# Moving the weights 16 bytes against the tensors that stream past them, on TensorE, in one diffusion-transformer layer

## The reference, cut to what matters

```python
proj = h @ w_in                        # 2048 -> 3072, latent and context tokens
u_f, u_x, u_g = jnp.split(proj, [D_FOURIER, D_FOURIER + D_LRU], axis=-1)
x_c = depthwise_conv(u_x, conv_w, conv_b, LRU_CONV // 2)
...
y = jnp.concatenate([y_fourier, y_lru], axis=-1) @ w_out      # 2048 -> 2048
x = x + gt1 * rms_norm(y, g_mix_post)
hx2 = modulate(rms_norm(x, g_ffn_pre), sh2, sc2)
up = depthwise_conv(hx2 @ w_up, conv_w, conv_b, FFN_CONV // 2)   # 2048 -> 11264
g, v = jnp.split(up, 2, axis=-1)
x = x + gt2 * rms_norm((jax.nn.gelu(g, approximate=True) * v) @ w_down, g_ffn_post)
```

## The kernel before, in words

| tensor | first byte | remainder |
|---|---|---|
| h_hi / h_lo | 20,192 / 52,960 | 224 |
| w_raw and w_lo / w_hi | 85,728 / 106,208 | 224 |
| hc_lo / hc_hi | 126,688 / 143,072 | 224 |
| t_lo / t_hi | 126,688 / 138,976 | 224 |
| sums1_lo / sums1_hi | 155,360 / 193,632 | 224 / 96 |
| act_hi / act_lo | 204,512 / 212,704 | 224 |
| xc and g parts (recurrence gates) | 165,600 and up / 190,176 and up | 224 |
| eo parts (weights) / m parts (stream), Fourier | 159,456 and up / 176,000 and up | 224 / 384 |
| p parts (weights) / tok parts (stream), Fourier | 184,192 and up / 167,744 and up | 384 / 320 to 376 |

## Time and profile before

### The profile page before, as it was taken

How to read it: one execution, slowest core, us unless ns; L and a number is a source line. 1 busy time by engine, 2 the same in 40 slices (tenths; PEclk the granted TensorE clock), 3 DMA queues, 4 the chain that set the end, 5 groups by cost and what they waited for, 6 DMA issues and landing times.

```text
span 2103.6 us, 28297 instructions
## 1 busy us (share of the span) xinstructions
PE 2071.2 (98%) x11682; PEld 1772.5 (84%) x11682; DVE 1529.6 (73%) x2202; ACT 811.6 (39%) x1077; POOL 78.7 (4%) x145
## 2 busy tenths in 40 slices
PE   7999999999999999999999999999999999999998
PEld 4678887888777888888889898898988889888887
DVE  5567978876988975867767676676766758577577
ACT  5346577543323442423324233332333424233243
POOL 0000000001110000000000000000000000000002
PEclk9999999999999999999999999999999999999999
DMA  9953424434876523333333333334233333232343
GB/s 394 408 204 110 154 96 161 137 109 173 323 277 225 181 90 134 100 128 111 110 130 101 138 103 103 129 101 140 100 120 121 100 130 100 91 101 101 100 172 109
DMA packets 86193, 311.19 MB, mean 148 GB/s; under 512 B 9456, under 2 KB 13552, under 8 KB 84016
## 3 DMA queue, kind: packets, MB, share of 16 engines
q1 hardware_dynamic: 67824, 243.09, 32.7%
q0 software_dynamic: 17424, 65.50, 9.1%
q10 hardware_dynamic: 816, 0.79, 0.1%
HBM read 300.95 MB, written 8.39 MB: 147 GB/s over the span
## 4 chain that ended last, share of the span: by engine, by line
PE 80%; DVE 2%; ACT 1%; DMA 1%; issue 0%; DVEq 0%; ACTq 0%
PE bank L988 26%; PE bank L990 26%; PE bank L989 26%; DMA w_raw<-in_stream 1%; PE bank L1099 1%; DVE acc L2167 0%; PE bank L1284 0%; DVE w_lo L1532 0%; ACT w_hi L602 0%; PE bank L1313 0%; PE bank L1194 0%; DVE acc L2139 0%; ACT lru_u L698 0%; DVE cv L1544 0%; DVE x L2193 0%
## 5 line engine op out<-in xcount | busy, mean ns | idle before, releaser
L988 PE MATMUL bank<-h_hi,w_hi 128*128 128x512 f32 (+1 forms) x1968 | 711.2, 361 | 4.2 <-ACT y_lru L671 1.2
L989 PE MATMUL bank<-h_lo,w_hi 128*128 128x512 f32 (+1 forms) x1968 | 708.6, 360 | 0.0
L990 PE MATMUL bank<-h_hi,w_lo 128*128 128x512 f32 (+1 forms) x1968 | 707.2, 359 | 0.0
L1532 DVE TENSOR_TENSOR w_lo<-w_raw,w_hi 128x1024 fp32r<-128x1024 f32 x260 | 316.0, 1222 | 157.9 <-ACT w_hi L602 157.8
L988 PEld LDWEIGHTS bank<-h_hi,w_hi 128*128 128x128 f32 x1968 | 372.3, 189 | 63.6 <-issue 11.9
L602 ACT ACTIVATE w_hi<-w_raw 128x1024 fp32r<-128x1024 f32 x260 | 273.0, 1056 | 389.1 <-DMA w_raw<-in_stream 389.0
L990 PEld LDWEIGHTS bank<-h_hi,w_lo 128*128 128x128 f32 x1968 | 372.1, 189 | 56.6
L989 PEld LDWEIGHTS bank<-h_lo,w_hi 128*128 128x128 f32 x1968 | 372.3, 189 | 49.0
L988 PE MATMUL bank<-act_hi,w_hi 128*128 128x512 f32 (+1 forms) x688 | 265.0, 385 | 1.7 <-DVE acc L2139 1.5
L990 PE MATMUL bank<-act_hi,w_lo 128*128 128x512 f32 (+1 forms) x688 | 264.2, 384 | 0.0
L989 PE MATMUL bank<-act_lo,w_hi 128*128 128x512 f32 (+1 forms) x688 | 264.2, 384 | 0.0
(11 more groups left out here) (340 smaller groups left out, 2711.4 us busy)
## 6 DMA issues: line engine op xcount, KB each, us to landing
w_raw<-in_stream SPq DMA_DIRECT2D x340, 512.0 KB, 3.5
ada_raw<-in_adabg POOLq DMA_DIRECT2D x112, 512.0 KB, 4.3
ada_raw<-in_ada SPq DMA_DIRECT2D x64, 512.0 KB, 13.5
x<-in_x_t SPq DMA_DIRECT2D x4, 1024.0 KB, 8.4
acc<-in_adabg SPq DMA_DIRECT2D x8, 512.0 KB, 6.1
x<-in_x_t POOLq DMA_DIRECT2D x4, 1024.0 KB, 9.4
x_kept_d<-x SPq DMA_DIRECT2D x4, 1024.0 KB, 5.6
c<-in_ctx_t SPq DMA_DIRECT2D x2, 1024.0 KB, 14.3
```

The source lines that it names most:

```text
L988: t.matmul(out, w, v, start=start, stop=False)
L989: t.matmul(out, w, v_l, start=False, stop=False)
L990: return t.matmul(out, w_l, v, start=False, stop=stop)
L1532: v.tensor_tensor(lo_unit(n), raw_unit(n), hi_unit(n).bitcast(F32), ALU.subtract).then_inc(lo_done, 1)
```

## The change

The tensors of the ring become flat, each with 8 values (32 bytes) more than five slots, and every use of a slot starts 4 values (`SKIP`, 16 bytes) further up. A space of 480 bytes before `w_hi` brings its slots to the remainder of `w_lo`'s. What lies behind `w_hi` on the left side moves up by 544 bytes, which is 512 and 32. `gap_to_act` shrinks from 1664 to 128 bytes. `ada_rows`, a buffer of 1 KB for the conditioning rows, becomes a view of `csq0`, the buffer of squares of the context tokens, so that `ada0_raw` moves down by that 1 KB less the 544.

```diff
+SKIP = 4
...
-        w_raw, w_lo = twice(ctx, "w_raw", "w_lo", [P, RING, UNIT])
-        w_hi = sbuf(ctx, "w_hi", [P, RING, UNIT], F32R)
+        w_raw, w_lo = twice(ctx, "w_raw", "w_lo", [P, RING * UNIT + 8])
+        sbuf(ctx, "gap_to_high", [P, 120])
+        w_hi = sbuf(ctx, "w_hi", [P, RING * UNIT + 8], F32R)
...
-                ada_rows = sbuf(s0, "ada_rows", [P, 2 * P])
+                ada_rows = csq0[:, 0, :]
...
-            sbuf(s, "gap_to_act", [P, 416])
+            sbuf(s, "gap_to_act", [P, 32])
...
-                return w_raw[:, SLOT[n], :]
+                return w_raw[:, ds(SKIP + UNIT * SLOT[n], UNIT)]
...
-                return w_hi[:, SLOT[n], :]
+                return w_hi[:, ds(SKIP + UNIT * SLOT[n], UNIT)]
...
-                return w_lo[:, SLOT[n], :]
+                return w_lo[:, ds(SKIP + UNIT * SLOT[n], UNIT)]
...
-            return w_raw[:, SUMS0, 0:NSUM], w_hi[:, SUMS0, 0:NSUM], w_lo[:, SUMS0, 0:NSUM]
+            return tuple(t[:, ds(SKIP + UNIT * SUMS0, NSUM)] for t in (w_raw, w_hi, w_lo))
...
-                a.activation(ada_rows[:, :], rows_bank(c)[:, 0:2 * P], ACT.Copy).then_inc(rows_copied, 1)
+                a.activation(ada_rows, rows_bank(c)[:, 0:2 * P], ACT.Copy).then_inc(rows_copied, 1)
```

## The result

The changed kernel takes 2121.44 us (median of three: 2120.11, 2121.44, 2125.28); its ratio to the kernel before is 1.0078, 95% interval 1.006 to 1.0096.

A forecast was written before the change was run, and what follows sets the result against it. TensorE's row of matmuls, busy 98%, was taken as the bound: 2 ns less on 9216 matmuls, other edits 0, made 2105.4 - 18.4 = 2087.0 us, plus 0.6 to the median, written 2088; range 2030 to 2128.

The forecast's parts named there:

- The failed step: Extended a 2 ns gain from short matmuls to the 6192 long ones, within 18 us less for 9216 matmuls.
- row (a): Last 18 matmuls of seven_products, one weight tensor 128 bytes lower: 118.3 ns each against 120, 1.7 ns on the mean.
- (b): Six 512-column steps right behind the matmuls with sums take 230 ns each, 3 ns above the steady 227.
- All other edits at 0 us: Ring passes, transfers and moved conditioning rows were taken as 0 us; the transfers' bounds were 0 and +10 us.
- the surplus: About 13 ns per matmul beyond its columns, absent at half clock; all of it would be 123 us over 9216 matmuls.
- the lost rhythm: 6192 long matmuls lose 3 to 5 ns each, wandering from 230: 2120 to 2132 us; chance 0.30 with settling higher.
- settled higher: Rhythm settles one short-kind surplus higher; half of 13.3 ns up would be +61 us; shares chance 0.30 with the lost rhythm.
- No change: Distance matters only above 16 bytes, or the rhythm settles again at 120 and 227 ns: 2106 us; chance 0.19.
- The large gain: Stream and loads stop meeting; half or all of the surplus goes, 61 or 123 us: 2044 or 1983 us; chance 0.20.

The follow-up runs named there:

- d0: The changed kernel's layout with weights at distance 0 from all streams, as in the kernel before; 2106.47 us, ratio 1.0007 to the kernel before.
- m128: As d0, but with weights 128 bytes below all streams; 2136.34 us in one run.
- p16: As d0, but with weights 16 bytes above all streams, act included; 2136.64 us, ratio 1.0146 to the kernel before.
- m64act: As d0, but with weights 64 bytes below h, hc and t, and act kept at distance 0; 2095.05 us, ratio 0.9948 to the kernel before.

## Why the prediction was wrong

**The failed step** is the one that took row (a), the 2 ns that short matmuls with sums gained at 128 bytes, over to the long ones ("I extend it to the long matmuls, for which the rows show only a worse value in transition; this is the weakest step"). It made 2 x 6192 = 12 us less of what became 6.1 ns more for each long matmul on `h` in the steady state, 0.1 ns for each on `act` in four down projections and 1.6 in six, and 14.7 us more in all. The row that was at hand, (b), pointed the other way; it was set aside since the steps had settled after six. But (b) was such a transition back to distance 0. At +16 there is nothing at 227 to return to: the steps settle at 233.3 within the first matmuls and stay.

**What held.** TensorE's pace was the bound, and the starts of successive matmuls told all. The short matmuls: 119.9 to 118.1 ns, the 2 ns forecast for them, 0.13 us in each of 40 turns. All other edits at 0 us: d0's ratio is 1.0007 (0.9998 to 1.0016), landing 3.5 us and 1055 ns a pass. That the surplus exists at the full clock only: m128's six steps of 427 ns. The first 125 us were 1.2 us shorter, for another reason than the change: seven steps of 427 ns at half the clock, five of them in the earlier trace rows, have no counterpart in the trace after, whose granted clock from 43 to 45.4 us is 1.00, and 7 x 0.2 is 1.4 us. With the stretch at 493 us, the trace before lost about 3 us to the clock that the trace after didn't, so the change costs nearer to 18 us than to 14.7 at an equal clock (an estimate).

**The rival that came true** is the lost rhythm, 2120 to 2132 us for a measured 2121.4. Its place was half right: 4224 long matmuls on `h`, not the 1968 on `act`. Its picture was half right too: the steps are uneven, from 231 to 235 ns, but they don't wander; they repeat in a pattern whose mean is 233.3, which is the other half of its case ("settled higher"). Its price of 3 to 5 ns was short of 6, and the two errors made up for each other. Neither it nor any other case gave the sign of the distance a part, though the change had both signs, +16 for `h` and -16 for `act`, `hc` and `t`; by p16 both at +16 would have cost 30 us.

**No change** fell by the trace and by p16 against d0. The Trainium skill, page "SBUF — State Buffer", section "Who interferes with whom", has TensorE's two read ports independent and never waiting. The runs disagree: with nothing but the weights' place moved by 16 bytes, a long step goes from 227.2 to 233.3 ns. The same page could be right in that neither port waits on another engine; no run here looked at that.

**The large gain** fell as well. Half of it exists for short steps, 113.4 of 120, but at 64 bytes and not at 16, and long ones never went under 226.7. The even rhythms, in which all steps are alike to 1 ns, have 113.3, 120 and 226.7 ns, which are 17, 18 and 34 times 6.67 ns: 16 cycles of 2.4 GHz, in which 64 bytes of a stream pass. 233.3 is 35 times as much, but it, 228.3, 229 and 117.3 to 118.7 are means of steps of several lengths (at -128 bytes 229 and 238 ns in turn), and these single steps are no multiples. So the surplus of 13.3 ns, which the prediction read as 32 cycles for 32 pieces of 16 bytes, may come in portions of 6.67, one or two of them in the even rhythms; the uneven ones leave it open. By the formula of the Trainium skill, page "TensorE: Matmul & The Clock Gate", section "Back-to-back issue gap", a long step would be 216 ns, as the prediction took it; the section gives that for an isolated matmul, and for a stream in which each has its load about 131 ns. The least here was 226.7, so neither holds in this kernel.

**Shown and open.** Shown: the distance between weights and stream sets the steady step, with its sign, for each length in its own way, and 256 bytes more make no difference at distance 0; the place of both together does not (32 bytes at distance 0, 64 bytes at -64); at -64 short matmuls have two steady rhythms, and what precedes decides; at -16 long ones have two. Argued only: that stream and weight load meet at parts of the 256 bytes and that one waits out a portion of 64 bytes; no run shows the meeting itself. Why +16 and -16 differ, and +64 and -64 for long steps alone, stays open, as do distances of 32, 96 and 160 bytes, and whether one-column matmuls in the right place could set the good rhythm on purpose, or taking them out keep it; none of these was tried.

## What to carry to other kernels

When TensorE runs without gaps and each matmul loads its own weights, compare the starts of successive matmuls for each shape, and treat the remainders of weights and stream by 256 as a parameter to be scanned in steps of 16 to 64 bytes; the sign counts, and a value from one column count says nothing for another. Read what a small misalignment settles to, not how it recovers in a trace in which the alignment comes back. Read more than one place of the trace: the same matmuls can run at another level 300 us later. And before two optima are put into one kernel, ask whether the work between them keeps a rhythm: here the combination gave 0.16% where the steps, taken one by one, had promised 0.95%.

## What the runs showed that was not expected

- The even rhythms at the full clock are multiples of 6.67 ns (113.3, 120 and 226.7), and at half the clock the steps are the columns alone (427 ns).
- The same matmuls with the same addresses go at 113.3 or 117.8 ns for hundreds of us, and long ones at -16 bytes at 226.7 or 228.3; in the traces of six kernels a change stands right behind the same 16 matmuls of one column.
- What a down projection at distance 0 leaves behind outlives 24 long matmuls at -64: the short ones behind them go at 117.8 instead of 113.4 (m64act).
- Weights 64 bytes below all streams, with no instruction changed, took 0.4% off a kernel in which TensorE was 98% busy.
